# Differential attention: who subtracts the low part of each head's weight slab

## The reference

```python
q = rope(rms_norm(q, q_g)); k = rope(rms_norm(k, k_g))
s = einsum(q_blk, k) * scale                      # two score maps a head
p = softmax(where(allowed, s, -inf))
a = p[:, :, 0] - lam * p[:, :, 1]
o = einsum(a, v)
o = rms_norm(o, sub_g) * (1.0 - lambda_init)      # after the last block
```

## Time and profile before

| | us |
|---|---|
| median of 3 runs | 2472.04 |
| profiled execution | 2476.54 |
| its span | 2474.8 |
| TensorE busy in the span | 2263.5 (91%) |
| VectorE busy | 1588.1 (64%) |
| ScalarE busy | 1295.7 (52%) |
| GpSimd busy | 312.0 (13%) |

### The profile page before, as it was taken

One profiled execution on the slowest core, in us unless ns is written; L12 is line 12 of the kernel. 1 busy time (PEld: TensorE's weight loads), 2 busy tenths in 40 slices (PEclk: granted clock), 3 DMA queues, 4 the chain that ended last, 5 costly groups with the idle time before them and its releaser, 6 DMA issues. The chain is left out here.

```text
span 2474.8 us, 30164 instructions
## 1 busy us (share of the span) xinstructions
PE 2263.5 (91%) x10164; PEld 1806.8 (73%) x10164; DVE 1588.1 (64%) x1753; ACT 1295.7 (52%) x1516; POOL 312.0 (13%) x403
## 2 busy tenths in 40 slices
PE   5888799899899999999439999999999999999995
PEld 4777577666566788888427888888888888888884
DVE  4677534444333434433428998889889888988983
ACT  5444334334222333321117777777777777777772
POOL 1332200200122000000131011101101110111000
PEclk8899799999899999999559999999999999999998
DMA  4110042311111233332738999999999999999983
GB/s 168 52 51 26 1 158 81 109 60 44 32 39 40 102 128 101 94 96 74 266 58 333 372 376 373 372 366 373 376 360 380 375 371 375 372 370 366 377 325 120
DMA packets 89714, 526.73 MB, mean 213 GB/s; under 512 B 13668, under 2 KB 14628, under 8 KB 38856
## 3 DMA queue, kind: packets, MB, share of 16 engines
q1 hardware_dynamic: 79720, 500.69, 53.7%
q0 software_dynamic: 9936, 25.28, 4.8%
HBM read 510.68 MB, written 25.99 MB: 217 GB/s over the span
## 5 line engine op out<-in xcount | busy, mean ns | idle before, releaser
L1851 DVE TENSOR_TENSOR moe_lo<-moe_raw,moe_hi 128x2048 fp32r<-128x2048 f32 x384 | 860.9, 2283 | 2.0 <-ACT moe_hi L1844 0.5
L1844 ACT ACTIVATE moe_hi<-moe_raw 128x2048 fp32r<-128x2048 f32 x384 | 735.6, 1918 | 155.1 <-PE bank L1862 155.0
L1860 PE MATMUL bank<-moe_hi,moe_XTh 128*128 128x512 f32 x1024 | 403.4, 394 | 4.6 <-DVE moe_lo L1851 4.6
L1862 PE MATMUL bank<-moe_hi,moe_XTl 128*128 128x512 f32 x1024 | 401.9, 392 | 0.0
L1861 PE MATMUL bank<-moe_lo,moe_XTh 128*128 128x512 f32 x1024 | 400.3, 391 | 0.0
L160 ACT ACTIVATE unit_hi<-unit_raw 128x1024 fp32r<-128x1024 f32 x120 | 126.7, 1059 | 295.6 <-DMA unit_raw<-in_w_units 280.6
L166 DVE TENSOR_TENSOR unit_lo<-unit_raw,unit_hi 128x1024 fp32r<-128x1024 f32 x120 | 146.3, 1223 | 195.0 <-ACT unit_hi L160 192.2
L1860 PEld LDWEIGHTS bank<-moe_hi,moe_XTh 128*128 128x128 f32 x1024 | 193.5, 189 | 43.6 <-DVE moe_lo L1851 5.4
L1862 PEld LDWEIGHTS bank<-moe_hi,moe_XTl 128*128 128x128 f32 x1024 | 192.5, 188 | 44.6
L1861 PEld LDWEIGHTS bank<-moe_lo,moe_XTh 128*128 128x128 f32 x1024 | 193.0, 188 | 43.2
L1860 PE MATMUL bank<-moe_hi,moe_aTh 128*128 128x512 f32 x512 | 204.2, 399 | 2.1 <-DVE moe_aTl L1955 2.1
(11 more groups left out here) (323 smaller groups left out, 3729.9 us busy)
## 6 DMA issues: line engine op xcount, KB each, us to landing
moe_raw<-in_w_moe SPq DMA_DIRECT2D x384, 1024.0 KB, 6.9
unit_raw<-in_w_units SPq DMA_DIRECT2D x120, 512.0 KB, 3.5
da_slab<-in_w_qkv SPq DMA_DIRECT2D x8, 1536.0 KB, 6.6
x_sb<-in_x SPq DMA_DIRECT2D x4, 512.0 KB, 5.1
yda_d<-y_daT SPq DMA_DIRECT2D x1, 2048.0 KB, 7.1
y_daT<-in_blocks_qk SPq DMA_DIRECT2D x1, 2048.0 KB, 7.9
y_daT<-yda_d SPq DMA_DIRECT2D x1, 2048.0 KB, 8.0
y_daT<-in_x SPq DMA_DIRECT2D x1, 2048.0 KB, 9.8
```

What stands on the lines that cost most here:

```text
L1844: nc.scalar.activation(HI[pos % 6][:], RAW[pos][:], ACT.Copy).then_inc(s_hi, 1)
L1851: nc.vector.tensor_tensor(LO[pos][:], RAW[pos][:], HI[pos % 6][:].bitcast(F32), ALU.subtract).then_inc(s_lo, 1)
L1860: nc.tensor.matmul(bank[:], xh[:, x], HI[ring][:, w], start=start and k == 0, stop=False)
L1862: mm = nc.tensor.matmul(bank[:], xl[:, x], HI[ring][:, w], start=False, stop=stop and k == 3)
```

## The change

`slab_lo` moves from VectorE's program to GpSimd's. Its arithmetic, tiles and semaphores stay; the wait becomes a `hold`. In VectorE's body it stood in each of the four steps. In GpSimd's body two chunks follow the rotations of step 2, and two come in step 3. In the prologue GpSimd does slab 0 before its first rotation, and one chunk of slab 1 behind each rotation.

```diff
+            def slab_lo(n, par, i):
+                hold(K, pool, s_wh, n * 4 + (i + 1))
+                nc.gpsimd.tensor_tensor(slo[par][:, i * 768:(i + 1) * 768], chunk(slab[par], i),
+                                        chunk(shi[par], i).bitcast(F32), ALU.subtract).then_inc(s_wl, 1)
+
@@ GpSimd's body and prologue @@
                         for t in projs[i][1:]:
                             rotate(h + 1, t)
+                    if more2 and i >= 2:
+                        for j in range(2 * i - 4, 2 * i - 2):
+                            slab_lo(h + 2, par, j)
                 o_rstd(h)
 
+            for i in range(TT):
+                slab_lo(0, 0, i)
             for i in range(TT):
                 rotate(0, i)
+                slab_lo(1, 1, i)
@@ VectorE's body and prologue @@
-            def slab_lo(n, par, i):
-                dve.wait_ge(s_wh, n * 4 + (i + 1))
-                nc.vector.tensor_tensor(slo[par][:, i * 768:(i + 1) * 768], chunk(slab[par], i),
-                                        chunk(shi[par], i).bitcast(F32), ALU.subtract).then_inc(s_wl, 1)
-
                     if more:
                         rope(h + 1, i)
-                    if more2:
-                        slab_lo(h + 2, par, i)
-                    elif more:
+                    if more and not more2:
                         unit_lo(K, dve, 0, i)
-            for i in range(TT):
-                slab_lo(0, 0, i)
             for i in range(TT):
                 rope(0, i)
-                slab_lo(1, 1, i)
```

## The result

The changed kernel takes 2506.66 us (median of 4 runs, 2505.43 to 2508.26) against 2470.75 us for the kernel before (4 runs, 2465.98 to 2472.45). The ratio is 1.0149, with a 95% interval of 1.0131 to 1.0166: 36 us slower. The forecast was 2511 in a range of 2497 to 2531.

What follows compares the result with a forecast made beforehand. The differential attention was taken as bound by TensorE, with holes. Loop delay 35.3, clock 0.1 and prologue 3.1 summed to 38.5 us slower, a median of 2511 us; own range 2501 to 2521, over the cases 2497 to 2531.

Steps and rivals of the forecast that it cites:

- The place of the loss: End of heads 0 to 5: `da_ors` waits behind four GpSimd subtractions; delay 6.85 us, net 5.88 a head, 35.3 in all.
- The subtraction's price: One 128x768 subtraction on GpSimd: 1.90 us plus 0.08 gap, with 1.56 as lower and 2.5 as upper end.
- the 612 and 1268 ns rows: Profiled GpSimd subtractions of 128x256 and 128x512, whose line gave 1.92 us for 128x768.
- VectorE's relief: Inside a head, TensorE's 0.69 and 0.28 us holes waiting for attention rows `a` close: 0.97 us gained a head.
- The clock: TensorE restarting at 1.2 GHz after six waits: 1.9 us each, net +0.1; as a rival +13, 2524 us, chance 0.10.
- The row of the prologue: TensorE's restart in the prologue: after 4.94 us idle, granted clock 0.51 until 36 us, 1.9 us of work lost.
- The prologue: Eight subtractions on GpSimd before the loop: 3.1 us together, from 0.9 to 7.2.
- The 1.0 us for three longer rounds: Prologue, slab 1: rotation plus subtraction take 4.40 us in a 4.08 us round, 0.32 too long, three times.
- Partly hidden: Rival: freed VectorE brings a head's last rotation forward by 3 us instead of 1; 26.5 us, 2499; chance 0.06.
- Disturbed subtractions: Rival: GpSimd's subtractions take 2.4 us or more, meeting VectorE's reads or slower on full tiles; 57 us, 2529; chance 0.12.

Runs made afterwards that it cites:

- The kernel with two late: Kernel before, with two of each head's four loop subtractions (chunks 2 and 3) on GpSimd ahead of `da_ors`, the rest on VectorE: 2484.96 us, ratio 1.0060.
- the kernel with all four behind: Changed kernel with the prologue's subtractions back on VectorE and each head's four on GpSimd moved behind o_rstd: 2488.69 us, ratio 1.0092.
- The kernel without any subtraction: Kernel before with the loop's subtractions left out on every engine (prologue kept on VectorE, low parts missing from the result): 2452.44 us, ratio 0.9937.
- The filled kernel: Changed kernel, prologue back on VectorE, TensorE filling its wait for da_on in heads 0 to 5 with 34 unused matmuls: 2492.51 us, ratio 1.0094.
- the spread kernel: Changed kernel, prologue back on VectorE, one GpSimd subtraction behind its rotation in steps 0 to 2, the fourth behind o_rstd: 2476.84 us, ratio 1.0037.
- With halves: The spread kernel with each GpSimd subtraction of 128x768 cut into two of 128x384: 2467.00 us, ratio 0.9996.

## Why the prediction was right

**The place of the loss.** Right. It was put at `da_ors` behind four subtractions, in six heads, and the rows after show it there. The kernel with two late gives the dose (3.07 against 6.58 us), and the kernel with all four behind shows that the wait follows the queue.

**The subtraction's price.** 1.90 us with a gap of 0.08 was taken. It is 1.805 us, and four start to end fill 7.08 us, so 1.77 each, without the gaps. The 1.90, taken from the line through the 612 and 1268 ns rows, was 5% too high; the Trainium skill's ratio of 1.96 (GPSIMD Engine Reference, Elementwise — side-by-side cycle accounting) with 1.87 us by 4%. The delay from the rotation to the scaling grew by 6.03 us instead of 6.85. This is the largest mis-sized term, 4.9 us in all.

**VectorE's relief.** 0.97 us a head was taken. The holes closed. From L386 to the next head's last rotation it is 27.72 us (134.24 to 161.96). With 2.5 us of low clock taken off that is 25.2, against 26.3 before (156.61 to 182.93): 1.1 us gained. The kernel without any subtraction shows that with the undisturbed rotation 1.9 us a head would be there. The changed kernel cannot collect the rotation's part, since it comes ahead of the long wait, as the prediction said.

**The clock.** A restart at the 1.2 GHz level behind all six waits was foreseen, at 1.9 us each and a net of +0.1. The filled kernel puts it at 2.5 us each, 15 us against 11.3 before: a net of +3.7. The row of the prologue was too cheap a model: behind these waits the 1.2 GHz level lasts 6.0 us, not under 4. The 11.3 is of one execution; how much it varies no run here shows.

**The prologue.** 3.1 us was taken; the traces show 1.4 to 1.9. The start was sized well: ScalarE's first read stands at 40.33 instead of 38.49, 1.8 us later where 2.0 was computed. The 1.0 us for three longer rounds was wrong: ScalarE's reads stand 4.16 us apart in both kernels, so a chunk of slab 1 fits into a round.

**The sum.** 6 x (6.03 - 1.1) + 3.7 + 1.4 = 34.7 us, against 34.6 in the trace and 35.9 by the medians. The forecast of 38.5 was 3.9 us above the trace and 2.6 above the medians. The subtraction (4.9) and the prologue (1.7) were overpriced; the clock (3.6) and VectorE's relief (0.8) were underpriced and took most of that back. That the total came so near is partly luck; without this it would have been 6.6 us too high, still inside the range.

**The rivals.** Partly hidden: the last rotation came forward by 1.1 us and not by 3. The clock: it cost 3.7 us more than before and not 13. Disturbed subtractions: not in the changed kernel (1797 to 1842 ns), where VectorE stands waiting, as argued. In the spread kernel it is VectorE that is disturbed. The prediction had looked at the disturbance in one direction only, from VectorE's reads on GpSimd's rotation. The other direction can be seen in the prologue of the changed kernel too, where it did not hold TensorE up:

```profile
31.77 7.16 POOL L485 TENSOR_TENSOR da_slab_lo<-da_slab,da_slab_hi 128x768 fp32r<-128x768 f32 x4 [17.19 <-ACT da_slab_hi L429]
...
33.92 1.47 DVE L580 TENSOR_TENSOR lamv<-lamv 128x1 f32<-128x1 f32 x1 [3.57 <-ACT lamv L459]
```

One number a partition, 0.15 us in the kernel before, takes 1.47 us: it begins beside the second subtraction and ends with it.

## What to carry to other kernels

An engine that is 70% idle is not a free place: ask what stands behind the new work in its queue, and who waits for that. Four subtractions of 1.8 us ahead of a result that had 0.5 us of slack made it 6 us later in each of six heads. And beside VectorE, GpSimd's elementwise work costs VectorE's time as well: put it where VectorE has nothing to read, or cut it small.

## What the runs showed of the hardware

A GpSimd subtraction of 128x768 held back until its end VectorE instructions with two inputs in SBUF (128x1: 0.15 us became 1.47; 128x512: 0.68 became 2.04) and a tensor_scalar of 128x2 fp32 from SBUF (0.168 became 1.69). With halves the last two were 1.23 and 0.96 us. Not touched were reductions of PSUM (0.56 and 0.69 us), a tensor_scalar out of PSUM (0.74) and a reciprocal of 128x2 in SBUF (0.15). One tensor_scalar of 128x1 in SBUF, begun 0.10 us behind the start of a subtraction, kept its 0.15 us, so not every tensor_scalar is held. The Trainium skill, GPSIMD Engine Reference, Specifications, names contention with VectorE instructions that have two SBUF inputs or run in a 2-port perf mode. For the first kind the runs agree, and show the wait lasting to the end of the GpSimd instruction; in which mode the 128x2 tensor_scalar ran no row shows. The other way, a rotation took 1.24 instead of 0.61 us beside a VectorE subtraction, and a subtraction 2.27 instead of 1.80 us when VectorE was ahead.

A wait of 6.7 us on TensorE was followed by 6.0 us at 1.2 GHz (134.24 to 140.2 us in the changed kernel), which cost 2.5 us of the period; 34 matmuls that nobody reads, put into the wait, bought it back.
